# Norms summed with tokens on partitions, 768-token tiles as two halves of 384 columns, and written-out TensorE loops in a three-block network

## What is computed

```
def rms_norm(x, g):
    xf = x.astype(jnp.float32)
    y = xf * lax.rsqrt(jnp.mean(xf * xf, axis=-1, keepdims=True) + EPS)
    return (y * g.astype(jnp.float32)).astype(x.dtype)

def sqrelu_mlp(h, w1, w2):
    return jnp.square(jax.nn.relu(h @ w1)) @ w2

hx = rms_norm(x, norm1_g[layer]) * (1 + mod_x[1]) + mod_x[0]
x = x + mod_x[2] * y_x
x = x + mod_x[5] * sqrelu_mlp(rms_norm(x, norm2_g[layer]) * (1 + mod_x[4]) + mod_x[3], mlp_w1[layer], mlp_w2[layer])
```

## Time and profile before

| | |
|---|---|
| median of 3 runs | 2670.71 us (2670.26 to 2671.92) |
| profiled execution | 2669.27 us |
| its span, first to last instruction | 2667.5 us |
| mean granted TensorE clock | 0.956 |
| PE, DVE, POOL, ACT busy | 92%, 56%, 43%, 36% |

### The profile page before, as it was taken

One profiled execution on the slowest core, in us unless ns is written; L12 is line 12 of the kernel. 1 busy time (PEld: TensorE's weight loads), 2 busy tenths in 40 slices (PEclk: granted clock), 3 DMA queues, 4 the chain that ended last, 5 costly groups with the idle time before them and its releaser, 6 DMA issues.

```text
span 2667.5 us, 31916 instructions
## 1 busy us (share of the span) xinstructions
PE 2443.4 (92%) x11638; PEld 1970.1 (74%) x11638; DVE 1489.1 (56%) x1987; ACT 972.6 (36%) x1519; POOL 1141.5 (43%) x857
## 2 busy tenths in 40 slices
PE   7999887999999988699989999797888889899999
PEld 6888776888888877466678888676644666688877
DVE  6856866737273745988452123479588443543433
ACT  4322334212121326577452233442434353432322
POOL 1533132535253522388544476344553331344444
PEclk6999998999999999799999999998999899999999
DMA  5433021424242321312222232132200110232323
GB/s 221 136 111 131 28 72 65 141 79 142 79 135 85 127 78 48 101 42 52 75 79 90 91 102 95 63 103 87 95 0 1 63 64 25 79 103 90 99 93 105
DMA packets 68822, 231.69 MB, mean 87 GB/s; under 512 B 8048, under 2 KB 10992, under 8 KB 68592
## 3 DMA queue, kind: packets, MB, share of 16 engines
q1 hardware_dynamic: 68720, 230.35, 26.7%
HBM read 219.57 MB, written 2.10 MB: 83 GB/s over the span
## 4 chain that ended last, share of the span: by engine, by line
PE 72%; DVE 11%; issue 8%; POOL 5%; ACT 3%; DMA 1%; SPq 0%; POOLq 0%; DVEq 0%; ACTq 0%
PE PS L676 53%; PE PS L694 8%; POOL HL L531 4%; PE PS L717 2%; DVE RD L2381 2%; PE PS L1152 1%; PE PS L976 1%; DVE ADJ L2013 1%; DVE SM L2365 1%; PE PS L1245 1%; PE PS L1141 1%; PE PS L751 0%; PE PS L1117 0%; PE PS L1160 0%; DMA EARLY<-adastream 0%
## 5 line engine op out<-in xcount | busy, mean ns | idle before, releaser
L531 POOL TENSOR_TENSOR HL<-RAW,HL 128x512 fp32r<-128x512 f32 x614 | 905.7, 1497 | 1316.8 <-ACT HL L1290 1316.5
L676 PE MATMUL PS<-HA,HL 128*128 128x512 f32 (+1 forms) x2592 | 556.9, 368 | 14.0 <-DVE VS L2484 4.6
L676 PE MATMUL PS<-HID,HL 128*128 128x512 f32 (+1 forms) x2832 | 565.6, 362 | 0.0
L676 PE MATMUL PS<-HB,HL 128*128 128x512 f32 (+1 forms) x2592 | 542.0, 361 | 0.0
L676 PEld LDWEIGHTS PS<-HID,HL 128*128 128x128 f32 x2832 | 478.8, 188 | 85.4
L676 PEld LDWEIGHTS PS<-HA,HL 128*128 128x128 f32 x2592 | 444.3, 190 | 106.8 <-issue 26.1
L676 PEld LDWEIGHTS PS<-HB,HL 128*128 128x128 f32 x2592 | 442.3, 188 | 77.1
L1290 ACT ACTIVATE HL<-RAW 128x1024 fp32r<-128x1024 f32 x307 | 323.1, 1053 | 475.0 <-PE PS L676 383.9
L2013 DVE CUSTOM_DVE_ANT_0 ADJ<-ADA,CB 128x1024 f32<-128x1024 f32 x160 | 269.1, 1682 | 9.2 <-DVE X L1935 2.7
L1935 DVE SCALAR_TENSOR_TENSOR X<-PS,MOD,X 128x256 f32<-128x256 f32 (+1 forms) x120 | 75.7, 658 | 334.7 <-PE PS L676 316.2
L694 PE MATMUL PS<-HA,HL 128*128 128x256 f32 (+1 forms) x576 | 138.7, 404 | 59.2 <-DVE HA L1916 44.0
(11 more groups left out here) (376 smaller groups left out, 2726.3 us busy)
## 6 DMA issues: line engine op xcount, KB each, us to landing
RAW<-wstream SPq DMA_DIRECT2D x307, 512.0 KB, 3.5
ADA<-adastream SPq DMA_DIRECT2D x80, 512.0 KB, 3.8
EARLY<-adastream SPq DMA_DIRECT2D x16, 512.0 KB, 14.5
QB<-QH SPq DMA_DIRECT2D x32, 128.0 KB, 2.3
X<-x_in SPq DMA_DIRECT2D x8, 384.0 KB, 6.4
QC<-QL SPq DMA_DIRECT2D x16, 128.0 KB, 2.3
out<-X SPq DMA_DIRECT2D x8, 256.0 KB, 2.3
X<-mem SPq DMA_DIRECT2D x1, 1024.0 KB, 5.6
```

The costliest lines, as they stand in the source:

```text
L531: a = pool.tensor_tensor(HL[:, t % RING, 1, half], RAW[:, t % RAW_RING, half], HL[:, t % RING, 0, half].bitcast(F32), ALU.subtract)
L676: mm = pe.matmul(bank(t % 2, r), w[:, wp, k * P:(k + 1) * P], a[:, ap, lo:hi], start=(k == 0 and (wp, ap) == (0, 0)), stop=(k == nk - 1 an ...
```

## The change

- **Sum over partitions.** `norm_sum` now multiplies each block of 128 tokens of `ACC` (as stationary operand) with one column of ones, so the sums come out with tokens on partitions, 6 columns in all (4 for x). The last chunk's squares are not added to `ACC`: they are summed from `SQ` by products of their own into the same columns. Ln, Exp and Newton work on 6 columns. `norm_spread` brings the root back to all partitions in PSUM banks 5 and 6: root column broadcast as stationary operand, identity as moving one.
- **Scaling.** DVE multiplies X by the gain and by the root, read from PSUM, in one operation (the factor -0.5/D moves into the gains). ACT makes one pass a chunk (`norm_high`), DVE adds the shift in the low part (`norm_low`). Four chunk buffers instead of two.
- **Fillers.** `keep_clock` issues products of 256 columns on constants into bank 4, whose result nobody reads, at three places of a norm (not in 0a).
- **Memory norm.** The memory's norm "2m" leaves 2a: its squares stand before the out1 tiles, its root is taken with 1b's, and its scaling stands in the last quarter of MLP 1.
- **Halves.** `parts` cuts a cx tile into columns 0 to 384 and 384 to 768, one bank each; the two k1 tiles keep 256 and 512. The residual of a cx tile becomes three pieces.
- **Pair.** `gemm_pair` waits for the second tile's bank only when its first product is due.
- **Loops.** PE's loops in both MLPs and the last FFN are written out; ACT's and DVE's stay.
- **ada.** PE computes 8 chunks at the start instead of 9, DVE one more; chunks 46 and 47 stand behind norm 0b; in MLP 0 the 12 chunks of a quarter stand at tiles 0 to 5 and 8 to 13 instead of 0 to 11.

```
-ADA_PE = 9
+ADA_PE = 8
+        def parts(slot, regions):
+            if regions == "cx":
+                return [(2 * slot, 0, NT // 2), (2 * slot + 1, NT // 2, NT)]
+            return [(2 * slot + (r == "x"), *REG[r]) for r in regions]
...
+            def keep_clock(n, bk=4):
+                for _ in range(n):
+                    pe.matmul(PS[:, bk, 0:NCTX], const(C_ONE), CST[:, 0:2, :].rearrange("p n m -> p (n m)"), start=True, stop=True)
+            def norm_sum(n, regions, squares=None):
+                squares = squares or regions
+                blocks, last = blocks_of(regions), blocks_of(squares)
+                pe.wait_ge(S("norm_acc"), of_norm(n, "acc", KC - (n != "0a")))
+                for b in blocks:
+                    mm = pe.matmul(PS[:, 5, b:b + 1], ACC[:, b * P:(b + 1) * P], const(C_ONE)[:, 0:1], start=(b == blocks[0]),
+                              stop=True, skip_group_check=(b != blocks[0]))
+                if n != "0a":
+                    keep_clock(2 if len(blocks) > 4 else 1)
+                    pe.wait_ge(S("norm_sq"), of_norm(n, "sq", KC))
+                for b in last if n != "0a" else ():
+                    mm = pe.matmul(PS[:, 5, b:b + 1], SQ[:, (KC - 1) % 2, b * P:(b + 1) * P], const(C_ONE)[:, 0:1],
+                                   start=False, stop=True, skip_group_check=True)
+                mm.then_inc(S("norm_sum"), 1)
+            def norm_spread(n, regions):
+                if n != "0a":
+                    keep_clock(2)
+                pe.wait_ge(S("norm_root"), of_norm(n, "root", 1))
+                for b in blocks_of(regions):
+                    bk, o = (5, b) if b < NCTX // P else (6, b - NCTX // P)
+                    mm = pe.matmul(PS[:, bk, o * P:(o + 1) * P], RS[:, b:b + 1].to_broadcast([P, P]), const(C_ID),
+                                   start=True, stop=True)
+                mm.then_inc(S("norm_sum"), 1)
+                if n != "0a":
+                    keep_clock(6 if n in ("0b", "1a") else 4)
...
@@ gemm_pair
-                banks_free(t + 1, q)
...
                     for tt in (t, t + 1):
+                        if k == order[0] and tt > t:
+                            banks_free(tt, q)
...
@@ mlp on PE
-                norm_sum(nid, regions)
-                with pe.Fori(0, MLP_QUARTERS) as q:
-                    quarter(q)
+                rows = "cx" if layer else regions
+                norm_sum(nid, rows, regions)
+                norm_spread(nid, rows)
+                for q in range(MLP_QUARTERS):
+                    quarter(q, t0 + 16 * q)
...
@@ DVE
+            def norm_scale(n, k, regions):
+                if k >= 4:
+                    dve.wait_ge(S("norm_lo"), of_norm(n, "lo", k - 3))
+                for r in regions:
+                    lo, hi = REG[r]
+                    c = "xc".index(r)
+                    a = dve.scalar_tensor_tensor(norm_buffer(k)[:, lo:hi], X[:, k, lo:hi], AT[:, k, c:c + 1],
+                                                 PS[:, 5 if r == "c" else 6, 0:hi - lo], ALU.mult, ALU.mult)
+                a.then_inc(S("norm_scaled"), 1)
+            def norm(n, regions, bias=None):
+                dve.wait_ge(S("norm_sum"), of_norm(n, "sum", 2))
+                for k in range(KC):
+                    norm_scale(n, k, regions)
+                    if k:
+                        norm_low(n, k - 1, regions, bias)
+                norm_low(n, KC - 1, regions, bias)
```

More of the change, by code:

```diff
@@ L191, in bank, with count, norm_buffer, blocks_of @@
             return PS[:, 2 * slot, 0:NCTX] if r == "c" else PS[:, 2 * slot + 1, 0:NX]
+        def parts(slot, regions):
+            if regions == "cx":
+                return [(2 * slot, 0, NT // 2), (2 * slot + 1, NT // 2, NT)]
+            return [(2 * slot + (r == "x"), *REG[r]) for r in regions]
         def span(regions):
             return REG[regions[0]][0], REG[regions[-1]][1]
-        NORMS = ["0a", "0b", "1a", "1b", "2a", "2b", "2c"]
         def of_norm(n, step, value):
-            order = [x for y in NORMS for x in ((y,) if y != "2a" or step not in ("sq", "acc") else ("2m", y))]
-            each = {"sum": 1, "rsqrt": 2}.get(step, KC)
-            return order.index(n) * each + value
+            order = ["0a", "0b", "1a", "1b", "2a", "2b", "2c"]
+            if step in ("sq", "acc"):
+                order.insert(3, "2m")
+            elif step in ("scaled", "hi", "lo"):
+                order.insert(4, "2m")
+            def count(x):
+                if step == "acc" and x not in ("0a", "2m"):
+                    return KC - 1
+                return {"sum": 2, "rsqrt": 2, "root": 1}.get(step, KC)
+            return sum(count(x) for x in order[:order.index(n)]) + value
+        def norm_buffer(k):
+            return (T1 if k % 4 < 2 else T2)[:, k % 2]
+        def blocks_of(regions):
+            lo, hi = span(regions)
+            return range(lo // P, hi // P)
         per = {"T": 16, "A": 8, "V": 8}
@@ L1318, in norm_root, with norm_high, norm @@
                 act.wait_ge(S("norm_sum"), of_norm(n, "sum", 1))
-                parts = [(RS[:, REG[r][0]:REG[r][1]], PS[:, 5 if r == "c" else 6, 0:REG[r][1] - REG[r][0]])
-                         for r in regions]
-                rsqrt(parts, D, "norm_rsqrt")
+                blocks = blocks_of(regions)
+                r = RS[:, blocks[0]:blocks[-1] + 1]
+                rsqrt([(r, PS[:, 5, blocks[0]:blocks[-1] + 1])], D, "norm_rsqrt")
                 act.wait_ge(S("norm_rsqrt"), of_norm(n, "rsqrt", 1))
-                lo, hi = span(regions)
-                act.activation(RS[:, lo:hi], RS[:, lo:hi], ACT.Exp, scale=-0.5).then_inc(S("norm_rsqrt"), 1)
-            def norm(n, regions, bias, root=True, between=None):
-                if root:
-                    norm_root(n, regions)
+                act.activation(r, r, ACT.Exp, scale=-0.5).then_inc(S("norm_rsqrt"), 1)
+            def norm_high(n, k, regions, bias):
+                act.wait_ge(S("norm_scaled"), of_norm(n, "scaled", k + 1))
+                for r in regions:
+                    lo, hi = REG[r]
+                    b = bias(k, "xc".index(r)) if bias else None
+                    f = dict(bias=b) if bias else {}
+                    a = act.activation(H(k)[:, 0, lo:hi], norm_buffer(k)[:, lo:hi], ACT.Identity if bias else ACT.Copy, **f)
+                a.then_inc(S("norm_hi"), 1)
+            def norm(n, regions, bias, between=None):
                 for k in range(KC):
@@ L1396, in _ @@
             act.wait_ge(S("dve_once"), ONCE["first_gains"])
-            norm("0a", "cx", shift((0, 0)), root=False, between=lambda: high(2))
+            norm("0a", "cx", shift((0, 0)), between=lambda: high(2))
             t = 0
@@ L1537, in _ @@
             t += 64
+            norm_root("1a", "cx")
             norm("1a", "cx", shift((1, 0)))
@@ L2301, in _ @@
             residual_tiles(t, "cx", (0, 2), "0a", "0b")
+            gains(0, 4, PC["n2g"])
+            norm_root("0b", "cx")
+            norm("0b", "cx", shift((0, 3)))
+            for i in (46, 47):
+                ada(i)
             modulation(0, 40, ADA_CHUNKS)
-            gains(0, 4, PC["n2g"])
-            norm("0b", "cx")
             t += 8
```

222 lines of the change are left out of this document (110 added, 112 removed).

## The result

The changed kernel takes 2612.98 us, median of 4 runs (2609.96 to 2614.86), against 2671.32 for the kernel before, run beside it: a ratio of 0.9784, 95% interval 0.9768 to 0.9799. The forecast was 2607 us, range 2592 to 2634. The profiled execution took 2614.8 us, of which the span is 2613.0, 54.5 less than before.

The account below looks back on a forecast made before the run. TensorE, busy 92% of the span, was taken as the bound. Savings of 45.3 + 1.5 + 11.0 + 6.6 = 64.4 us from 2669.27 gave 2604.9; with 2 us added the forecast was 2607 us, range 2592 to 2634.

Parts of the forecast that it names:

- Six norms, 45.3 us: Norms 0b, 1a, 1b, 2a, 2b, 2c with their pairs: a shorter chain of full-width operations saves 45.3 us.
- The first norm, 1.5: Norm 0a at the kernel's start: its new chain saves 1.5 us, ends -1 and +3.
- Halves, 11.0: 768-column tiles: 384-column products at 173.3 ns replace the 256/512 mixture's slower 177.0, saving 11.0 us, bounds 0 and 14.
- Seams, 6.6: PE's waits between MLP quarters and in the FFN: awaiting the pair's second bank later saves 6.6 of 8.0 us.
- Loops written out, 0: PE's loops in the MLPs and FFN: writing them out gains nothing beyond the seams, unless the jump itself costs something.
- the rival that ended on the other side: PE's written-out MLP and FFN code arrives late: 64 us lost if each product costs 11 ns more; chance 0.03.
- The memory norm's place, 0: MLP 1's last quarter: the moved memory-norm work, even doubled to 1.8 us a tile, fits beside DVE's own operations.
- The stretches behind the norms, 0: Code left unchanged from 2a to 2b and 2b to 2c: assumed to keep its length, 0 us.
- The allowance of 2 us: Whole kernel: 2 us added to the forecast for links and waits counted short.
- the clock still falls: Rival in the six norms: PE's clock drops despite fillers, costing 32 us, giving 2639; chance 0.13.
- halves bring nothing: Rival for the 768-column tiles: 384-column products save 0 us, giving 2618, or 2621; chance 0.09.
- other engine limits the pairs: Rival in the norms' pairs: DVE's two operations a chunk cost 1.3 times the rows, 24 us, giving 2631; chance 0.05.

Follow-up runs that it names:

- experiment 5: The changed kernel with PE's loops over the MLP quarters and the FFN groups kept as before: 2611.53 us, ratio 0.9793.
- 6: The changed kernel with 256- and 512-column tiles, PE's loops and the early wait for the pair's second bank as before: 2622.62 us, ratio 0.984.
- experiment 4: The changed kernel with the 768-column tiles cut into 256 and 512 columns again and the residual in two pieces: 2615.56 us, ratio 0.9809.
- experiment 9: The kernel before with only the halves of 384 and the residual in three pieces: 2659.67 us, ratio 0.997.
- experiment 2: The changed kernel with the memory norm's scaling, high and low parts moved into the second eight tiles of MLP 1's last quarter: 2617.18 us, ratio 0.9808.
- experiment 11: The changed kernel run again without any edit: 2611.22 us, ratio 0.9788.

## Why the forecast was right

**Six norms, 45.3 us: right, 45.1.** The windows were forecast at 27.5, 28.1, 20.6, 19.4, 19.0 and 19.3 and are 27.34, 29.27, 19.59, 19.61, 19.23 and 19.00. The chain of 0b was T+10.4 and is T+10.3; the 12 one-column records took 1.50 us (1.3 forecast), the spread 1.60 (up to 1.4), the fillers 2.76 (2.8). 1a is 1.2 over for the stretch at the lower clock (28.11 without it, in experiment 5); 1b is 1.0 under, so that the sum came out closer than its terms. Without fillers the norms would have given 27.5.

**The first norm, 1.5: small by 1.4.** The pair starts at 54.27 (55 to 57 forecast) and ends at 73.70. With starts of the first pair 5.7 us apart in code that is the same up to there, the term can't be sized better from single profiles.

**Halves, 11.0: the mechanism right, the size 8.0, the account wrong.** Products of 384 columns cost 173.7 ns with or without loops, as I had interpolated. What was not seen is that the pace of the mixture is not fixed by the instructions: of its four quarters in MLP 0, turns of one loop before and in 6, three were slow before, one in experiment 4, none in 6. (Whether it also changes between executions of one kernel no profile shows.) Halves are worth 8.0 us against the kernel before and some 2.5 against the changed kernel with the old tiles (1.8 in MLP 0, 0.7 before 0b). What decides the mixture's pace was not found; neither loop nor straight code does. The 2.5 is read from single profiles, and the two medians, 2.6 apart, do not confirm it beyond their spread. By the Trainium skill's rule of one fixed cost for each product ("TensorE: Matmul & The Clock Gate", section "Wait — 56ns, not 53.3ns?") halves should bring nothing: that agrees with the fast pace (173.6 for the mixture, 173.7 for halves), and the slow one, 177.0, has no place in it.

**Seams, 6.6: 5.9.** MLP 0 is 2.9 us shorter in the changed kernel than with halves alone (experiment 9, 521.7), 0.97 a seam as forecast. MLP 1 is 1.9 shorter than before when the memory norm is out of the way (experiment 2, 340.1; 2.1 forecast), the FFN 1.1 (1.5 forecast).

**Loops written out, 0: not refuted in the sum, and not nothing.** In two kernels with loops one jump of three in MLP 0 cost 2.8 and 3.0 us, and low clock behind it; in the kernel before and in 9, none. The forecast named this possibility ("if the jump back itself costs something") and priced it at nothing. The Trainium skill, "Runtime: NRT & Kernel Launch", section "Instruction fetch mechanics", says that a taken branch may stall, and straight code is fetched ahead; the waits agree, as does the straight code's even pace, against the rival that ended on the other side.

**The memory norm's place, 0: wrong by 1.4.** The step that failed for this term is "1.8 fits beside the tile's own two DVE operations": the sum of the work does fit, but the queue has an order. A low part of HID that PE waits for at the turn from the first to the second eight stands behind the memory norm's passes (experiment 2).

**The stretches behind the norms, 0: wrong by 6.** This is the largest error and no step of the prediction, since it took for granted that an untouched stretch keeps its length. The heads did not: in the kernel before, products of head 0 that took 1.7 us longer at the low clock went with one long head less; the changed kernel did not have them in either of its profiles and takes 7.2 us longer over the heads (144.0 against 136.8), up to 3.4 of which differs between executions of the same code (experiment 11). The change is not shown to be what moved the low clock: experiments 5 and 6 have the new norms and the low clock in head 0. Just ahead of them and behind them it is 1.1 and 1.0 shorter. The 0.7 us between 2b and 2c have no explanation here.

The account of the profiled executions closes: 2604.9 was the sum, and halves 3.0, seams 0.7, the memory norm's place 1.4, the untouched stretches 6.0 and the six norms 0.2 on top, less 1.4 for the first norm, are 9.9: 2614.8, the profiled execution. The allowance of 2 us had covered a fifth of it.

Of the rivals, "the clock still falls" is partly true (two stretches of six; the row that it rested on held two-column products, not one-column ones), "halves bring nothing" is refuted by experiment 9, no other engine limits the pairs by more than forecast, and the written-out code is not late (its products of 384 columns start 173.3 ns apart).

## What to carry to other kernels

Price a moved operation by its place in the queue of the engine that takes it, not by whether the engine has the time. Where two engines slow each other down in a loop, the loop can fall into short and long turns, and a shift of 2 us in its first turn can change how many are long: several us are then won or lost with nothing changed in the loop, so compare stretches before crediting an edit. And do not price a slow pace as a fixed cost from one kernel's profile: the next kernel may not have it even without the change.

## What the runs showed of the hardware

- One-column products of 128 rows cost 125 ns a record (12 in 1.50 us) at full clock, nearly as much as 128-column ones (12 in 1.60, 133 ns). With fillers of 256 columns between them, 5.0 us in all in norm 0b, the clock stayed at 1.00 there in five of ten profiles and was low for 3.4 us in the others; without, it was 0.78 and the norm 4.0 us longer.
- Products that alternate between 256 and 512 columns have two steady paces: starts 173.3 ns apart in the mean (mostly 117 and 230) or 176.7 (113 to 120 and 232 to 241). Equal products of 384 at full clock have one in all ten profiles that contain them, 173.3.
- DVE's pass of 512 columns takes 0.69 us alone and 1.5 to 1.75 beside GpSimd; GpSimd's own takes 1.27 alone and mostly 1.6 to 1.8 beside DVE's.
- A loop's jump on TensorE's queue mostly costs nothing that can be seen: 2 of 28 in four profiles cost 2.8 and 3.0 us.
